# Two transformer blocks on one core: moving operands read backwards, and each chunk at another distance from its weights

## Chip, cores and metric

The kernel runs on one core of one Trainium2 chip. The metric is the device time of one execution in microseconds (us), from the first to the last instruction and what lies around it; lower is better. Two runs of the kernel before gave 3431.12 and 3433.68 us (median 3432.4).

## The reference

The reference computes two stacks of two layers each, on 512 tokens of width 1024, batch 1, everything in float32. In short:

```python
# first stack, per layer
proj = h @ w_in[l]                                    # 1024 -> 2594 columns
mixed = concat([nsa_mixer(...), gla_mixer(...), pool_mixer(...)])
h = layer_norm(ALPHA * h + mixed @ w_out[l], ...)
ff = square(relu(h @ w_up[l])) @ w_down[l]            # 1024 -> 4096 -> 1024
h = layer_norm(ALPHA * h + ff, ...)
# second stack, per layer
h = h + 0.5 * rms_norm(swiglu(rms_norm(h), ffn_wi, ffn_wo))   # 1024 -> 2 x 2816 -> 1024
h = h + rms_norm(attention(rms_norm(h)))              # dilated heads in layer 0, windowed GQA in layer 1
h = h + 0.5 * rms_norm(swiglu(rms_norm(h), ffn_wi, ffn_wo))
h = h + rms_norm((p @ ple_proj) * sigmoid(rms_norm(h) @ ple_gate))
```

Nearly all the arithmetic is in the dense products, which is where the change works.

## The kernel before

Everything is kept transposed: features lie on the 128 partitions, and the 512 tokens lie along the free dimension. The hidden state h is 8 chunks of 128 features. A dense product is therefore a sum over chunks kc: the stationary operand is a 128x128 block of weights, the moving operand is chunk kc of the activations with its 512 tokens (2048 bytes in each partition), and the result fills one PSUM bank of 512 float32.

The products are done in the type float32r, which rounds its operands. To keep float32 accuracy each operand is split in two: a high part (the value rounded to float32r) and a low part (the value minus the high part). Each product then takes three matmuls: high weights by high activations, high weights by low activations, low weights by high activations. This is `piece` (L870 to L876), the helper through which nearly all dense work goes; `abreast` (L910 to L928) does the same for the first tiles behind a norm, where the chunks of x come one at a time, with the three matmuls on L918, L919 and L925.

**Activations.** Three buffers hold split activations: `x` (8 chunks; input of the projections and of the first half of each feed-forward, and also the mixer's output in the first stack), `mid` (22 chunks; the hidden layer of the feed-forwards) and `px` (2 chunks; the embedding, inside x's memory). In the attention stages of the second stack `ao` and `bo` play the part of mid. Each chunk holds the 512 high values and behind them the 512 low values, so a chunk is 4096 bytes in each partition. ScalarE (ACT) writes the high part with a copy (L1589, L1606, L1672, L1803, L1850, L1861, L1881), VectorE (DVE) the low part by a subtraction (`lo_of` L2042, L2071, L2095, L2583).

**Weights.** The host lays all weights out as a stream of units of 128x1024 float32: 8 blocks of 128 columns, so block kc begins kc times 512 bytes into its unit. SyncE fetches them in order into 4 buffers `raw`; ACT makes the high part `wh` (L1549) and DVE the low part `wl` in the place of raw (L2026). Ten units go into a buffer apart (`wh_apart`, `wl_apart`), so that more of them are ready when a norm ends.

**Where things lie.** Buffers have hand-made addresses. `x` begins at byte 32896, a chunk and a weight unit are multiples of 512 bytes, and two lines pad `mid` and `bo` so that they too begin at the same residue:

```python
place[0] += (x_at - place[0]) % 512
mix_at = place[0]
mid = at("mid", [P, FF2C, 2, S], F32R)
```

So in the kernel before the first byte of every moving row of 2048 bytes and the first byte of every block of weights have the same address modulo 512.

**Order of the work.** Each engine has its own program written out by hand, with semaphores between them. TensorE runs through the units; in the mixer stages the small matmuls of the attention are woven in between the dense ones by plans (`plan_n`, `plan_a`, `plan_b`). At the end of each layer part a norm needs the whole result, and the first tiles behind it run `abreast`.

Of the kernel before, what the change touches and what calls it, by code (L numbers as in the profile page):

```python
# [25 lines left out]
P = 128  # L26
S = 512
# [10 lines left out]
BIG_NEG = -1.0e30  # L38
FLOOR = -1.0e20


# [347 lines left out]
def build(nc, stream, x_t, p_t, small, vecs, tab1, tab_a, tab_b, consts, out):  # L389
    n_units = stream.shape[0]  # L390
    with ExitStack() as ctx:
        place = [16512]

        def at(name, shape, dt=F32, offset=None):
# [5 lines left out]
            return nc.alloc_sbuf_tensor_at(name, shape, dt, offset=offset)  # L400

        def sem(name):
            s = ctx.enter_context(nc.semaphore(name))
            return s
# [3 lines left out]
        x_at = place[0]  # L408
        x = at("x", [P, DC, 2, S], F32R)
        y_at = place[0]  # L410
        y = at("y", [P, DC, S])
        px = at("px", [P, 2, 2, S], F32R, offset=x_at + 6 * 2 * S * 4)
        raw = [at(f"raw{i}", [P, UNIT]) for i in range(4)]
# [13 lines left out]
        mix_at = place[0]  # L427
        mid = at("mid", [P, FF2C, 2, S], F32R)
        assert place[0] <= 229368, place[0]
# [438 lines left out]
        def _(pe):  # L868
            c = Count(pe)

            def piece(dst, u, col, src, kc, start, stop):

                hi, lo = high_of(u)[:, col:col + P], low_of(u)[:, col:col + P]
                pe.matmul(dst, hi, src[:, kc, 0, :], start=start, stop=False)  # L874
                pe.matmul(dst, hi, src[:, kc, 1, :], start=False, stop=False)  # L875
                return pe.matmul(dst, lo, src[:, kc, 0, :], start=False, stop=stop)  # L876

# [32 lines left out]
            def abreast(u, t, kc, width, summed=True):  # L910


                if t == 0:
                    c.wait(x_hi)
                at_ = slice(kc * P, kc * P + P)
                hi, lo = high_of(u + t)[:, at_], low_of(u + t)[:, at_]
                dst = bank[c.homes[t][0]][:, :]
                pe.matmul(dst, hi, x[:, kc, 0, :], start=kc == 0, stop=False)  # L918
                pe.matmul(dst, lo, x[:, kc, 0, :], start=False, stop=False)  # L919
                if t < width - 1:  # L920
                    return
                c.wait(x_ready)
                for i in range(width):
                    dst, hi = bank[c.homes[i][0]][:, :], high_of(u + i)[:, at_]
                    mm = pe.matmul(dst, hi, x[:, kc, 1, :], start=False, stop=kc == 7)  # L925
# [610 lines left out]
        def _(act):  # L1536
# [47 lines left out]
            def layer_norm(g, b, to_x, after=None, wide=False):  # L1584
                for k in range(DC):
                    c.wait(normed)
                    bias = vec[:, b + k:b + k + 1]
                    if to_x:
                        act.activation(x[:, k, 0, :], prod[k % 2][:, :], ACT.Identity, bias=bias).then_inc(x_hi, 1)  # L1589
# [79 lines left out]
            for k in range(DC):  # L1669
                if k % 2 == 0:  # L1670
                    act.wait_ge(h_in[k // 2], 16)
                act.activation(x[:, k, 0, :], h[:, k, :], ACT.Copy).then_inc(x_hi, 1)  # L1672
            split(2)
            act.wait_ge(consts_in, 48)

            for layer in range(DEPTH):
# [47 lines left out]
                for stage, k in plan_n(BY_TWO if layer else BY_ONE):  # L1724
# [40 lines left out]
                    elif stage == "mixed":  # L1765
                        if k == 0:
                            c.wait(go_out)
                            c.wait(pool_read, 2)
                        ch = (GO, GO + 1, GO + 2, PU, PU + 1)[k]
                        act.activation(x[:, 3 + k, 0, :], proj[:, ch, :], ACT.Copy).then_inc(mx_hi, 1)  # L1770
                    elif stage == "exps":
                        exps(*k)
                    elif stage == "blocks":
                        copy_blocks(*k)
                    elif stage == "shift":
                        c.tick("group1")
                        act.wait_ge(blk_turned, c.n["group1"])
                        act.activation(tmp[1][:, :], bank[6][:, :], ACT.Copy).then_inc(blk_read, 1)
                    elif stage == "out":
                        act.wait_ge(o_done, 12 * layer + 4 * k + 4)  # L1780
                        act.activation(x[:, k, 0, :], bank[7][:, :], ACT.Copy).then_inc(ot_hi, 1)
                c.tick("shifted", DC)
# [13 lines left out]
                def up4(i, counts=()):  # L1796
                    for k in range(4):
# [40 lines left out]
            def ffn2(embed=False):  # L1838
                def two(i, counts=()):
                    for k in range(2):  # L1840
# [8 lines left out]
                        c.wait(pair_made)  # L1849
                        act.activation(mid[:, i * 2 + k, 0, :], prod[k][:, :], ACT.Copy).then_inc(mid_hi, 1)  # L1850

# [6 lines left out]
                if embed:  # L1858
                    c.wait(p_in, 16)
                    for k in range(2):  # L1860
                        act.activation(px[:, k, 0, :], pf[:, k, :], ACT.Copy).then_inc(p_hi, 1)  # L1861
                    c.wait(p_ready, 2)
# [28 lines left out]
            def mixer_a():  # L1891
                c.start(banks_mixer)
                for stage, k in plan_a():
# [22 lines left out]
                    elif stage == "out":  # L1916
                        out_hi(ungrouped(ao[:, k, 0, :]), grouped_src(bank[7][:, :]), k)
                rest(1)
# [9 lines left out]
            def mixer_b():  # L1928
                c.start(banks_mixer)
                for stage, k in plan_b():  # L1930
# [21 lines left out]
                    elif stage == "out":  # L1952
                        out_hi(bo[:, k, 0, :], bank[7][:, :], 4 + k)
                rest(4)
# [62 lines left out]
        def _(dve):  # L2017
# [27 lines left out]
            def layer_norm(g, to_x, wide=False):  # L2045
# [22 lines left out]
                for k in range(DC):  # L2068
                    if to_x:
                        c.wait(x_hi)  # L2070
                        dve.scalar_tensor_tensor(x[:, k, 1, :], prod[k % 2][:, :], vec[:, g + 8 + k:g + 9 + k],  # L2071
                                                 x[:, k, 0, :].bitcast(F32), ALU.add, ALU.subtract).then_inc(x_ready, 1)
                        c.tick("made x_ready")
# [18 lines left out]
            def low_part(g, k):  # L2092

                c.wait(x_hi)
                dve.scalar_tensor_tensor(x[:, k, 1, :], h[:, k, :], vec[:, g + k:g + k + 1],  # L2095
                                         x[:, k, 0, :].bitcast(F32), ALU.mult, ALU.subtract).then_inc(x_ready, 1)
                c.tick("made x_ready")
# [268 lines left out]
            for k in range(DC):  # L2366
                c.wait(x_hi)
                lo_of(x[:, k, 1, :], h[:, k, :], x[:, k, 0, :], x_ready)
            split(2)
# [8 lines left out]
            for layer in range(DEPTH):  # L2378
                c.start(banks_first)
                for stage, k in plan_n(BY_TWO if layer else BY_ONE):  # L2380
# [46 lines left out]
                    elif stage == "mixed":  # L2427
                        ch = (GO, GO + 1, GO + 2, PU, PU + 1)[k]
                        c.wait(mx_hi)
                        lo_of(x[:, 3 + k, 1, :], proj[:, ch, :], x[:, 3 + k, 0, :], x_ready)  # L2430
                    elif stage == "values_in":
# [16 lines left out]
                    elif stage == "out_lo":  # L2448
                        c.wait(ot_hi)
                        dve.tensor_tensor(x[:, k, 1, :], bank[7][:, :], x[:, k, 0, :].bitcast(F32),  # L2450
                                          ALU.subtract).then_inc(ot_ready, 1)
# [25 lines left out]
                def up4(i, counts=()):  # L2477
                    for k in range(4):
# [42 lines left out]
            def ffn2(embed=False):  # L2521
                def two(i, counts=()):
                    for k in range(2):
# [7 lines left out]
                        c.wait(mid_hi)  # L2531
                        lo_of(mid[:, i * 2 + k, 1, :], prod[k][:, :], mid[:, i * 2 + k, 0, :], mid_ready)

# [5 lines left out]
                if embed:  # L2539
                    for k in range(2):  # L2540
                        c.wait(p_hi)
                        lo_of(px[:, k, 1, :], pf[:, k, :], px[:, k, 0, :], p_ready)
                for k in range(DC):
# [72 lines left out]
            def mixer_a():  # L2616
                trig(grouped(tba[:, A_COS:A_COS + S]), grouped(tba[:, A_SIN:A_SIN + S]), regrouped(rs_in[:, :]))
                c.start(banks_mixer)
                for stage, k in plan_a():
# [29 lines left out]
                    elif stage == "out_lo":  # L2649
                        out_low(ungrouped(ao[:, k, 1, :]), grouped_src(bank[7][:, :]), ungrouped(ao[:, k, 0, :]), k)  # L2650
                rest(1)
# [19 lines left out]
            def mixer_b():  # L2671
                trig(tbb[:, B_COS:B_COS + S], tbb[:, B_SIN:B_SIN + S], rs_in[:, :])
                c.start(banks_mixer)
                for stage, k in plan_b():
# [247 lines left out]
```

## Time and profile before

| | us |
|---|---|
| runs, not profiled | 3431.12 and 3433.68, median 3432.4 |
| the profiled execution, its own time | 3430.66 |
| its span, first to last instruction | 3428.8 |
| TensorE matmul busy | 3317.4, 97% |
| VectorE busy | 1836.8, 54% |
| ScalarE busy | 1241.6, 36% |

The mean granted clock of TensorE is 0.988 of full speed. The busy time of a matmul covers its whole way through the array, and matmuls overlap: one of 512 columns is shown as 390 ns long while the next begins some 227 ns after it. So the distance from start to start tells the pace, and the busy time does not.

### The profile page before, as it was taken

What the parts mean: (1) busy time and instruction counts of PE and PEld (TensorE: products, weight loads), DVE (VectorE), ACT (ScalarE), POOL (GpSimd) and SP (SyncE); (2) the same over time, 40 slices, a digit from 0 to 9 for tenths busy, and PEclk for the clock granted to TensorE, in tenths of its full rate; (3) what the DMA queues carried; (4) which work ended last, traced back from release to release, by engine and by line L of the source; (5) the groups of instructions that cost most, each with busy time, mean ns of one, the idle gap of its engine ahead of it and who ended that gap; (6) DMA issues with size and microseconds to landing.
All of it is one profiled execution on the core that took longest, in us unless ns stands there. A gap on an engine that the chain in (4) does not pass through costs nothing.

```text
span 3428.8 us, 42531 instructions
## 1 busy us (share of the span) xinstructions
PE 3317.4 (97%) x16570; PEld 2633.9 (77%) x16570; DVE 1836.8 (54%) x2932; ACT 1241.6 (36%) x1878; POOL 342.3 (10%) x244
## 2 busy tenths in 40 slices
PE   9999999999899999999999999999999989999997
PEld 6667888776688887888777778887788876688886
DVE  5776334567752446443566664435644357654436
ACT  3354222424442324332333342324432235532324
POOL 0310000212100020000233100000000012100001
PEclk9999999999999999999999999999999999999999
DMA  4102222311122222223322122232222321122232
GB/s 162 62 32 74 96 95 98 128 62 50 50 85 94 98 98 81 98 97 104 107 74 68 63 81 96 98 105 93 86 96 94 105 94 39 61 98 98 98 105 80
DMA packets 81431, 300.35 MB, mean 88 GB/s; under 512 B 9040, under 2 KB 9040, under 8 KB 80640
## 3 DMA queue, kind: packets, MB, share of 16 engines
q1 hardware_dynamic: 78624, 284.20, 24.8%
q0 software_dynamic: 1568, 11.98, 0.9%
q8 instruction: 103, 1.69, 0.2%
q10 hardware_dynamic: 1088, 2.10, 0.2%
q14 instruction: 48, 0.39, 0.0%
HBM read 296.14 MB, written 2.10 MB: 87 GB/s over the span
## 4 chain that ended last, share of the span: by engine, by line
PE 88%; DVE 6%; ACT 3%; issue 1%; POOL 1%; DMA 1%; ACTq 0%; DVEq 0%; POOLq 0%
PE bank L874 25%; PE bank L876 25%; PE bank L875 24%; PE bank L918 2%; PE bank L925 2%; PE bank L919 2%; DVE wl L2026 1%; PE bank L1411 1%; ACT sc L1710 1%; PE bank L1423 1%; PE bank L1175 1%; PE bank L1156 1%; ACT wh L1549 1%; PE bank L1466 1%; PE bank L1114 1%
## 5 line engine op out<-in xcount | busy, mean ns | idle before, releaser
L874 PE MATMUL bank<-x,wh 128*128 128x512 f32 x2632 | 1053.7, 400 | 14.8 <-DVE h L2470 5.7
L876 PE MATMUL bank<-x,wl 128*128 128x512 f32 x2632 | 1027.3, 390 | 0.0
L875 PE MATMUL bank<-x,wh 128*128 128x512 f32 x2632 | 1026.1, 390 | 0.0
L1549 ACT ACTIVATE wh<-raw 128x1024 fp32r<-128x1024 f32 x528 | 558.0, 1057 | 1171.6 <-PE bank L876 1083.6
L2026 DVE TENSOR_TENSOR wl<-raw,wh 128x1024 fp32r<-128x1024 f32 x528 | 677.7, 1284 | 567.4 <-ACT wh L1549 566.0
L874 PEld LDWEIGHTS bank<-x,wh 128*128 128x128 f32 x2632 | 494.9, 188 | 135.9 <-issue 29.4
L876 PEld LDWEIGHTS bank<-x,wl 128*128 128x128 f32 x2632 | 494.6, 188 | 105.4
L875 PEld LDWEIGHTS bank<-x,wh 128*128 128x128 f32 x2632 | 495.7, 188 | 98.4 <-issue 3.4
L874 PE MATMUL bank<-mid,wh 128*128 128x512 f32 x1216 | 474.9, 391 | 0.5 <-DVE wl L2026 0.5
L876 PE MATMUL bank<-mid,wl 128*128 128x512 f32 x1216 | 473.1, 389 | 0.0
L875 PE MATMUL bank<-mid,wh 128*128 128x512 f32 x1216 | 473.1, 389 | 0.0
L874 PEld LDWEIGHTS bank<-mid,wh 128*128 128x128 f32 x1216 | 228.3, 188 | 49.5 <-DVE wl L2026 1.3
L875 PEld LDWEIGHTS bank<-mid,wh 128*128 128x128 f32 x1216 | 228.3, 188 | 48.4 <-issue 1.0
L876 PEld LDWEIGHTS bank<-mid,wl 128*128 128x128 f32 x1216 | 228.3, 188 | 47.2
L2165 DVE TENSOR_TENSOR prod<-bank,rs_in 128x512 f32<-128x512 f32 x88 | 60.8, 691 | 231.7 <-PE bank L876 231.7
L2042 DVE TENSOR_TENSOR mid<-prod,mid 128x512 f32 (+1 forms) x152 | 104.8, 690 | 88.3 <-ACT mid L1850 85.5
L677 POOL TENSOR_TENSOR acc<-sq,sq 128x512 f32<-128x512 f32 x8 | 11.2, 1397 | 1299.2 <-ACT sq L1655 1299.2
L918 PE MATMUL bank<-x,wh 128*128 128x512 f32 x200 | 85.9, 429 | 46.9 <-ACT x L1606 23.8
L2482 DVE TENSOR_TENSOR prod<-tmp,bank 128x512 f32<-128x512 f32 x64 | 44.0, 687 | 142.9 <-ACT tmp L1800 142.9
L1850 ACT ACTIVATE mid<-prod 128x512 f32 (+1 forms) x88 | 55.6, 632 | 174.6 <-DVE prod L2530 174.6
L1800 ACT ACTIVATE tmp<-bank 128x512 f32<-128x512 f32 x64 | 38.2, 596 | 178.5 <-PE bank L876 178.5
L2165 DVE TENSOR_TENSOR tmp<-bank,rs_in 128x512 f32<-128x512 f32 x88 | 60.8, 691 | 59.7 <-PE bank L876 58.6
(340 smaller groups left out, 3294.5 us busy)
## 6 DMA issues: line engine op xcount, KB each, us to landing
raw<-stream SPq DMA_DIRECT2D x528, 512.0 KB, 3.3
raw_apart<-stream SPq DMA_DIRECT2D x10, 512.0 KB, 3.6
sm<-small POOLq DMA_DIRECT2D x2, 2144.0 KB, 10.6
tb<-tab POOLq DMA_DIRECT2D x2, 1728.0 KB, 14.8
h<-x_t ACTq DMA_DIRECT2D x4, 512.0 KB, 6.8
out_t<-h SPq DMA_DIRECT2D x8, 256.0 KB, 2.1
tba<-tab_a POOLq DMA_DIRECT2D x1, 1152.0 KB, 8.5
pf<-p_t POOLq DMA_DIRECT2D x2, 512.0 KB, 3.9
```

Source lines behind the costliest of these rows:

```text
L874: pe.matmul(dst, hi, src[:, kc, 0, :], start=start, stop=False)
L875: pe.matmul(dst, hi, src[:, kc, 1, :], start=False, stop=False)
L876: return pe.matmul(dst, lo, src[:, kc, 0, :], start=False, stop=stop)
L918: pe.matmul(dst, hi, x[:, kc, 0, :], start=kc == 0, stop=False)
L919: pe.matmul(dst, lo, x[:, kc, 0, :], start=False, stop=False)
L925: mm = pe.matmul(dst, hi, x[:, kc, 1, :], start=False, stop=kc == 7)
L1549: act.activation(high_of(n)[:, :], raw_of(n)[:, :], ACT.Copy).then_inc(hi_done, 1)
L1850: act.activation(mid[:, i * 2 + k, 0, :], prod[k][:, :], ACT.Copy).then_inc(mid_hi, 1)
L2026: dve.tensor_tensor(low_of(n)[:, :], raw_of(n)[:, :], high_of(n)[:, :].bitcast(F32), ALU.subtract).then_inc(split_done, 1)
L2042: dve.tensor_tensor(dst, src, hi.bitcast(F32), ALU.subtract).then_inc(done, 1)
L2165: free(dve.tensor_tensor(dst, bank[c.peek()][:, :], rs_in[:, :], ALU.mult))
L2482: free(dve.tensor_tensor(prod[k % 2][:, :], tmp[k % 2][:, :], b[:, :], ALU.mult))
```

## The change

It edits three things, all about where and in which order the split activations lie; no instruction is added, removed or moved on any engine, and the sequences of instructions of TensorE, VectorE, ScalarE, GpSimd and SyncE are the same but for line numbers.

1. The 512 tokens of each part are stored in reverse order in x, mid, px, ao and bo, and every dense matmul reads them with a step of minus one element, from the last byte of the row to the first. The columns arrive in the array in the same order of tokens as before, so the PSUM banks and all that reads them are as they were. What writes x, px, ao and bo writes backwards; what writes mid reads its source backwards and writes forwards.
2. The chunks of x and px are 16 bytes longer than their data (X_GAP, 4 elements), those of mid 32 bytes (MID_GAP, 8 elements). Chunk kc therefore begins 16 kc bytes (x) or 32 kc bytes (mid) past the residue that its block of weights has. ao and bo get no gap.
3. The buffers behind x are shifted so that they keep x's residue modulo 512, and the feed-forward's buffer apart, which lies inside mid's memory, moves by 192 bytes.

```diff
+X_GAP, MID_GAP = 4, 8
...
+        def staggered(name, chunks, gap, offset=None):
+
+            t = at(name, [P, chunks, 2 * S + gap], F32R, offset)
+            return t[:, :, 0:2 * S].rearrange("p k (e s) -> p k e s", e=2)
+
...
-        x = at("x", [P, DC, 2, S], F32R)
+        x = staggered("x", DC, X_GAP)
+        place[0] += (x_at - place[0]) % 512
...
-        px = at("px", [P, 2, 2, S], F32R, offset=x_at + 6 * 2 * S * 4)
+        px = staggered("px", 2, X_GAP, x_at + 6 * (2 * S + X_GAP) * 4)
...
-        mid = at("mid", [P, FF2C, 2, S], F32R)
+        mid = staggered("mid", FF2C, MID_GAP)
...
-        apart_at = [mix_at + 6 * 2 * S * 4, y_at]
+        apart_at = [mix_at + 6 * (2 * S + MID_GAP) * 4, y_at]
...
-                pe.matmul(dst, hi, src[:, kc, 0, :], start=start, stop=False)
-                pe.matmul(dst, hi, src[:, kc, 1, :], start=False, stop=False)
-                return pe.matmul(dst, lo, src[:, kc, 0, :], start=False, stop=stop)
+                pe.matmul(dst, hi, src[:, kc, 0, ::-1], start=start, stop=False)
+                pe.matmul(dst, hi, src[:, kc, 1, ::-1], start=False, stop=False)
+                return pe.matmul(dst, lo, src[:, kc, 0, ::-1], start=False, stop=stop)
...
-                act.activation(x[:, k, 0, :], h[:, k, :], ACT.Copy, scale=vec[:, g + k:g + k + 1]).then_inc(x_hi, 1)
+                act.activation(x[:, k, 0, ::-1], h[:, k, :], ACT.Copy, scale=vec[:, g + k:g + k + 1]).then_inc(x_hi, 1)
...
-                        act.activation(mid[:, i * 4 + k, 0, :], prod[k % 2][:, :], ACT.Copy).then_inc(mid_hi, 1)
+                        act.activation(mid[:, i * 4 + k, 0, :], prod[k % 2][:, ::-1], ACT.Copy).then_inc(mid_hi, 1)
...
-                        lo_of(mid[:, i * 4 + k, 1, :], prod[k % 2][:, :], mid[:, i * 4 + k, 0, :], mid_ready)
+                        lo_of(mid[:, i * 4 + k, 1, :], prod[k % 2][:, ::-1], mid[:, i * 4 + k, 0, :], mid_ready)
...
-                        out_low(bo[:, k, 1, :], bank[7][:, :], bo[:, k, 0, :], 4 + k)
+                        out_low(bo[:, k, 1, ::-1], bank[7][:, :], bo[:, k, 0, ::-1], 4 + k)
```

The other edits of the diff put the same `::-1` at the three matmuls of `abreast` and at the remaining writers of x, px, ao and bo (ACT and DVE), and reverse the source at the second writer of mid.

## Rows read from the trace of the kernel before

**Rows 1.** The page, parts 1 and 2: busy time by engine, granted clock, DMA.
```profile
PE 3317.4 (97%) x16570; PEld 2633.9 (77%) x16570; DVE 1836.8 (54%) x2932; ACT 1241.6 (36%) x1878; POOL 342.3 (10%) x244
...
PEclk9999999999999999999999999999999999999999
...
DMA packets 81431, 300.35 MB, mean 88 GB/s; under 512 B 9040, under 2 KB 9040, under 8 KB 80640
```
**Rows 2.** The page, part 4: the chain that ended last, by engine and by line.
```profile
PE 88%; DVE 6%; ACT 3%; issue 1%; POOL 1%; DMA 1%; ACTq 0%; DVEq 0%; POOLq 0%
```
**Rows 3.** The page, part 5: groups of the dense matmuls and the splits.
```profile
L874 PE MATMUL bank<-x,wh 128*128 128x512 f32 x2632 | 1053.7, 400 | 14.8 <-DVE h L2470 5.7
L875 PE MATMUL bank<-x,wh 128*128 128x512 f32 x2632 | 1026.1, 390 | 0.0
L1549 ACT ACTIVATE wh<-raw 128x1024 fp32r<-128x1024 f32 x528 | 558.0, 1057 | 1171.6 <-PE bank L876 1083.6
L2026 DVE TENSOR_TENSOR wl<-raw,wh 128x1024 fp32r<-128x1024 f32 x528 | 677.7, 1284 | 567.4 <-ACT wh L1549 566.0
L874 PE MATMUL bank<-mid,wh 128*128 128x512 f32 x1216 | 474.9, 391 | 0.5 <-DVE wl L2026 0.5
```
**Rows 4.** Smaller groups by form: L874 on other buffers, L918 on x.
```profile
L918 PE MATMUL bank<-x,wh 128*128 128x512 f32 x200 | 85.9, 429 | 46.9 <-ACT x L1606 23.8 <-ACT x L1589 12.2 <-ACT x L1672 6.9
...
L918 PE MATMUL bank<-x,wh_apart 128*128 128x512 f32 x64 | 27.3, 426 | 0.0
L874 PE MATMUL bank<-bo,wh 128*128 128x512 f32 x64 | 26.8, 419 | 0.2 <-DVE bo L2583 0.2
...
L874 PE MATMUL bank<-ao,wh 128*128 128x512 f32 x32 | 14.1, 441 | 2.9 <-DVE ao L2583 2.7
...
L874 PE MATMUL bank<-px,wh 128*128 128x512 f32 x16 | 7.1, 442 | 0.0
...
L874 PE MATMUL bank<-px,wh_apart 128*128 128x512 f32 x16 | 6.2, 389 | 0.0
```
**Rows 5.** Timeline of PE, an undisturbed stretch: start us, length us, engine, instruction.
```profile
499.83 0.39 PE L874 MATMUL bank<-x,wh 128*128 128x512 f32 x1
500.06 0.39 PE L875 MATMUL bank<-x,wh 128*128 128x512 f32 x1
...
502.78 0.39 PE L875 MATMUL bank<-x,wh 128*128 128x512 f32 x1
```
**Rows 6.** Timeline of PE's weight loads in the same stretch.
```profile
499.83 0.19 PEld L875 LDWEIGHTS bank<-x,wh 128*128 128x128 f32 x1
500.06 0.19 PEld L876 LDWEIGHTS bank<-x,wl 128*128 128x128 f32 x1
```
**Rows 7.** Timeline of PE behind a norm, at half clock.
```profile
1303.39 0.76 PE L918 MATMUL bank<-x,wh 128*128 128x512 f32 x1 [4.69 <-ACT x L1606]
...
1304.38 0.63 PE L918 MATMUL bank<-x,wh_apart 128*128 128x512 f32 x1
1304.81 0.63 PE L919 MATMUL bank<-x,wl_apart 128*128 128x512 f32 x1
...
1307.37 0.63 PE L918 MATMUL bank<-x,wh 128*128 128x512 f32 x1
```
**Rows 8.** Stretches: busy us (x) of PE, PEld, DVE, ACT, POOL; PEclk, DMA share, GB/s.
```profile
500.00:503.00 3.00, 3.00 (x14) 2.46 (x14) 0.71 (x2) 0.25 (x1) 0.00 (x0) 1.00 0.00 1
1303.00:1307.00 4.00, 3.61 (x9) 2.86 (x10) 3.72 (x6) 3.94 (x7) 0.00 (x0) 0.50 0.02 4
```
**Rows 9.** Timeline of PE: dense matmuls behind a group of small ones.
```profile
720.57 0.50 PE L874 MATMUL bank<-x,wh 128*128 128x512 f32 x1
720.91 0.40 PE L875 MATMUL bank<-x,wh 128*128 128x512 f32 x1
...
721.84 0.39 PE L876 MATMUL bank<-x,wl 128*128 128x512 f32 x1
...
722.52 0.39 PE L876 MATMUL bank<-x,wl 128*128 128x512 f32 x1
```
**Rows 10.** Writers of ao and bo: instruction, count, ns min/median/max, first and last start.
```profile
L1881 ACT ACTIVATE ao<-bank x4: 597/597/597, 1802.1 to 1971.8; 128x512 fp32r<-128x512 f32 x4
L2583 DVE TENSOR_TENSOR ao<-bank,ao x4: 680/680/683, 1806.2 to 1972.6; 128x512 fp32r<-128x512 f32 x4
...
L1881 ACT ACTIVATE bo<-bank x8: 572/574/597, 2848.3 to 2961.2; 128x512 fp32r<-128x512 f32 x8
L2583 DVE TENSOR_TENSOR bo<-bank,bo x8: 685/692/692, 2848.9 to 2962.5; 128x512 fp32r<-128x512 f32 x8
```
**Rows 11.** Waits of PE, longest first: us in total, times, longest.
```profile
PE bank L918 <- ACT x L1606: 23.8, 6, 4.7
PE bank L918 <- ACT x L1589: 12.2, 3, 4.3
```

More of the change, by code:

```diff
@@ L917, in abreast @@
                 dst = bank[c.homes[t][0]][:, :]
-                pe.matmul(dst, hi, x[:, kc, 0, :], start=kc == 0, stop=False)
-                pe.matmul(dst, lo, x[:, kc, 0, :], start=False, stop=False)
+                pe.matmul(dst, hi, x[:, kc, 0, ::-1], start=kc == 0, stop=False)
+                pe.matmul(dst, lo, x[:, kc, 0, ::-1], start=False, stop=False)
                 if t < width - 1:
@@ L924, in abreast @@
                     dst, hi = bank[c.homes[i][0]][:, :], high_of(u + i)[:, at_]
-                    mm = pe.matmul(dst, hi, x[:, kc, 1, :], start=False, stop=kc == 7)
+                    mm = pe.matmul(dst, hi, x[:, kc, 1, ::-1], start=False, stop=kc == 7)
                     if kc == 7:
@@ L1588, in layer_norm @@
                     if to_x:
-                        act.activation(x[:, k, 0, :], prod[k % 2][:, :], ACT.Identity, bias=bias).then_inc(x_hi, 1)
+                        act.activation(x[:, k, 0, ::-1], prod[k % 2][:, :], ACT.Identity, bias=bias).then_inc(x_hi, 1)
                         c.tick("affine")
@@ L1671, in _ @@
                     act.wait_ge(h_in[k // 2], 16)
-                act.activation(x[:, k, 0, :], h[:, k, :], ACT.Copy).then_inc(x_hi, 1)
+                act.activation(x[:, k, 0, ::-1], h[:, k, :], ACT.Copy).then_inc(x_hi, 1)
             split(2)
@@ L1769, in _ @@
                         ch = (GO, GO + 1, GO + 2, PU, PU + 1)[k]
-                        act.activation(x[:, 3 + k, 0, :], proj[:, ch, :], ACT.Copy).then_inc(mx_hi, 1)
+                        act.activation(x[:, 3 + k, 0, ::-1], proj[:, ch, :], ACT.Copy).then_inc(mx_hi, 1)
                     elif stage == "exps":
@@ L1780, in _ @@
                         act.wait_ge(o_done, 12 * layer + 4 * k + 4)
-                        act.activation(x[:, k, 0, :], bank[7][:, :], ACT.Copy).then_inc(ot_hi, 1)
+                        act.activation(x[:, k, 0, ::-1], bank[7][:, :], ACT.Copy).then_inc(ot_hi, 1)
                 c.tick("shifted", DC)
@@ L1849, in two @@
                         c.wait(pair_made)
-                        act.activation(mid[:, i * 2 + k, 0, :], prod[k][:, :], ACT.Copy).then_inc(mid_hi, 1)
+                        act.activation(mid[:, i * 2 + k, 0, :], prod[k][:, ::-1], ACT.Copy).then_inc(mid_hi, 1)
                 c.start(banks_gated)
@@ L1860, in ffn2 @@
                     for k in range(2):
-                        act.activation(px[:, k, 0, :], pf[:, k, :], ACT.Copy).then_inc(p_hi, 1)
+                        act.activation(px[:, k, 0, ::-1], pf[:, k, :], ACT.Copy).then_inc(p_hi, 1)
                     c.wait(p_ready, 2)
@@ L1916, in mixer_a @@
                     elif stage == "out":
-                        out_hi(ungrouped(ao[:, k, 0, :]), grouped_src(bank[7][:, :]), k)
+                        out_hi(ungrouped(ao[:, k, 0, ::-1]), grouped_src(bank[7][:, :]), k)
                 rest(1)
@@ L1952, in mixer_b @@
                     elif stage == "out":
-                        out_hi(bo[:, k, 0, :], bank[7][:, :], 4 + k)
+                        out_hi(bo[:, k, 0, ::-1], bank[7][:, :], 4 + k)
                 rest(4)
@@ L2070, in layer_norm @@
                         c.wait(x_hi)
-                        dve.scalar_tensor_tensor(x[:, k, 1, :], prod[k % 2][:, :], vec[:, g + 8 + k:g + 9 + k],
-                                                 x[:, k, 0, :].bitcast(F32), ALU.add, ALU.subtract).then_inc(x_ready, 1)
+                        dve.scalar_tensor_tensor(x[:, k, 1, ::-1], prod[k % 2][:, :], vec[:, g + 8 + k:g + 9 + k],
+                                                 x[:, k, 0, ::-1].bitcast(F32), ALU.add, ALU.subtract).then_inc(x_ready, 1)
                         c.tick("made x_ready")
@@ L2094, in low_part @@
                 c.wait(x_hi)
-                dve.scalar_tensor_tensor(x[:, k, 1, :], h[:, k, :], vec[:, g + k:g + k + 1],
-                                         x[:, k, 0, :].bitcast(F32), ALU.mult, ALU.subtract).then_inc(x_ready, 1)
+                dve.scalar_tensor_tensor(x[:, k, 1, ::-1], h[:, k, :], vec[:, g + k:g + k + 1],
+                                         x[:, k, 0, ::-1].bitcast(F32), ALU.mult, ALU.subtract).then_inc(x_ready, 1)
                 c.tick("made x_ready")
@@ L2367, in _ @@
                 c.wait(x_hi)
-                lo_of(x[:, k, 1, :], h[:, k, :], x[:, k, 0, :], x_ready)
+                lo_of(x[:, k, 1, ::-1], h[:, k, :], x[:, k, 0, ::-1], x_ready)
             split(2)
@@ L2429, in _ @@
                         c.wait(mx_hi)
-                        lo_of(x[:, 3 + k, 1, :], proj[:, ch, :], x[:, 3 + k, 0, :], x_ready)
+                        lo_of(x[:, 3 + k, 1, ::-1], proj[:, ch, :], x[:, 3 + k, 0, ::-1], x_ready)
                     elif stage == "values_in":
@@ L2449, in _ @@
                         c.wait(ot_hi)
-                        dve.tensor_tensor(x[:, k, 1, :], bank[7][:, :], x[:, k, 0, :].bitcast(F32),
+                        dve.tensor_tensor(x[:, k, 1, ::-1], bank[7][:, :], x[:, k, 0, ::-1].bitcast(F32),
                                           ALU.subtract).then_inc(ot_ready, 1)
@@ L2531, in two @@
                         c.wait(mid_hi)
-                        lo_of(mid[:, i * 2 + k, 1, :], prod[k][:, :], mid[:, i * 2 + k, 0, :], mid_ready)
+                        lo_of(mid[:, i * 2 + k, 1, :], prod[k][:, ::-1], mid[:, i * 2 + k, 0, :], mid_ready)
                 c.start(banks_gated)
@@ L2541, in ffn2 @@
                         c.wait(p_hi)
-                        lo_of(px[:, k, 1, :], pf[:, k, :], px[:, k, 0, :], p_ready)
+                        lo_of(px[:, k, 1, ::-1], pf[:, k, :], px[:, k, 0, ::-1], p_ready)
                 for k in range(DC):
@@ L2649, in mixer_a @@
                     elif stage == "out_lo":
-                        out_low(ungrouped(ao[:, k, 1, :]), grouped_src(bank[7][:, :]), ungrouped(ao[:, k, 0, :]), k)
+                        out_low(ungrouped(ao[:, k, 1, ::-1]), grouped_src(bank[7][:, :]), ungrouped(ao[:, k, 0, ::-1]), k)
                 rest(1)
```

## The prediction

> **What bounds the kernel now.** I read the busy shares first. TensorE is busy 97% of the span, and the granted clock shows 9 tenths or more in every slice [rows 1]. The chain of work that ended last agrees: 88% of it is PE, 6% DVE, 3% ACT, with almost nothing for DMA [rows 2]. The groups then say which work that is: the three lines of `piece` on x and on mid, with hardly any idle time before them (14.8 us before 2632 matmuls of L874) [rows 3]. The makers of the weights are paced by TensorE and not the other way: ACT sits idle 1171.6 us before its splits, 1083.6 of it until a matmul on L876 has ended, and a unit costs ACT 1.06 us and DVE 1.28 us, while its 24 matmuls take 24 x 0.227 = 5.4 us [rows 3]. So if one dense matmul gets cheaper, nearly all of it should reach the end.
>
> What does a dense matmul cost? Not its 390 ns, which overlap. In an undisturbed stretch 13 steps lie between 499.83 and 502.78 us: 2.95 / 13 = 226.9 ns each [rows 5]. The waits of TensorE elsewhere are short (23.8 and 12.2 us in all for the longest two, both the first chunks behind a norm) [rows 11].
>
> **How much of this 227 ns could be lost time.** Behind a norm the kernel shows the same matmul at half clock (PEclk 0.50, that is 1.2 GHz, after TensorE had stood idle 4.69 us for the norm [rows 7]; 1.00, that is 2.4 GHz, in the undisturbed stretch) [rows 8]. There 7 steps take 1307.37 - 1304.38 = 2.99 us, 427 ns each [rows 7]. 512 columns at 1.2 GHz are 426.7 ns: at half clock a step is its columns and nothing else. At full clock the same 512 columns are 213.3 ns, and the step is 226.7: 13.4 ns are lost in each, 32 cycles, only when the array runs fast. Something that is fast enough at half clock is too slow at full clock.
>
> What it might be shows in two places. The weight load of the next matmul starts in the same hundredth of a microsecond as the moving stream of the present one [rows 5, 6], so both are reading SBUF side by side. And the loss is not the same everywhere: behind a group of small matmuls the first 4 full steps take 721.84 - 720.91 = 0.93 us, 232.5 ns each, and then 3 steps take 722.52 - 721.84 = 0.68 us, 226.7 each, with the same operands' buffers and the same residues of their addresses [rows 9]. A fixed price of each instruction would not depend on how the two streams stand to each other in time. I take this as a sign, no proof, that the two reads hinder each other and that the loss depends on which addresses they are at when. The change alters just that: the direction in which the moving row is walked, and its distance to the weights.
>
> **The change part by part.**
>
> Count of matmuls it touches: L874 has 2632 (x), 1216 (mid) [rows 3], 64 (bo), 32 (ao), 16 + 16 (px) [rows 4], together 3976; L875 and L876 have as many each, so 11,928. `abreast` has 200 + 64 on L918 [rows 4] and as many on each of its other lines, 792. Sum 12,720. Of these, some run at half clock, where nothing is lost: the mean clock of 0.988 means 2.4% of 3428.8 us, 82 us, at most 82 / 0.427 = 190 matmuls. Others stand first behind small matmuls, where the step is 0.34 us (720.57 to 720.91 [rows 9]) for another reason: the mean of L874 on x is 10 ns above that of L875 [rows 3], 26 us in all, or about 240 such places at 0.11 us. I count 12,720 - 430 = about 12,300.
>
> Price for each step at full clock. Lower end: all lost time goes, 13.4 ns, -165 us. Upper end: each step becomes as the disturbed ones, 232.5 ns, +5.8 ns, +71 us; I see no row that would bear out more. The nearest row for "another relation of the two reads" is that of rows 9, but it is on the bad side, and the kernel's relation is one among many, so some distances will be better and some worse. Two things pull to the better side. Walking both in one direction, if the load walks from its last column, makes them meet less often than walking against each other; and 8 distances of 16 bytes (22 of 32 in mid) mean that no matmul repeats one bad relation for the whole product. I take half of the loss away: 220.1 ns, -6.6 x 12,300 = -81 us.
>
> The Trainium skill says the opposite in "SBUF — State Buffer", section "Who interferes with whom": the moving operand and the weight load have independent read ports and TensorE never waits on anyone. "TensorE: Matmul & The Clock Gate", part 1, gives a warm step as N / 2.4 + about 2.5 ns, which is 215.8 for 512 columns. The trace agrees with its cold step (427) and not with its warm one (226.7); it would give the change nothing if the ports were all there is, and -10.9 x 12,300 = -134 us if the excess over its figure is what the change removes.
>
> The writers. The reversed stores and loads of ACT and DVE add no instruction. The nearest rows: for ao, ACT reads its bank with steps of 128 elements and takes 597 ns, against 572 to 597 for bo, which reads straight; DVE takes 680 against 685 to 692 [rows 10]. So order costs these engines nothing beyond noise; at most 25 ns on each of about 100 chunk writes behind norms, where TensorE waits, 2.5 us. I take 0.
>
> Moved buffers and the gaps add no work. No queue or wait changes place. What is late next if steps shrink by 3%: the split of a unit (1.28 us on DVE) against 5.3 us of matmuls still has room, and the fetches run at a mean of 88 GB/s [rows 1] with peaks that TensorE nowhere waits for long [rows 11]. The waits behind norms stay as they are.
>
> **Sum.** Profiled execution 3430.7 us, less 81, is 3350; the median of the runs is 1.7 us above the profiled one. I predict 3350 us.
>
> **Rivals.**
>
> *All of the loss goes.* The new relation never meets, and the step falls to nearly its columns, 216 ns: -10.7 x 12,300 = -132 us, 3299 us. For it: the half-clock rows show that the loss can be absent. Against it: that is at another ratio of time to column, and the new distances are many, so some should still meet.
>
> *The loss is not a read conflict.* If 32 cycles are a fixed price of changing weights, hidden at half clock, then direction and distance change nothing: 3431 us. For it: the steps on x and on mid, on the high and the low part, are all the same 227 ns, with a stability that a conflict would not need to have. Against it: the 232.5 of rows 9. But before, every operand had the same residue, so sameness is what a conflict would show too.
>
> *The distances are worse than the common one.* Before, all operands had one residue, and the step locked at 226.7 after a few matmuls; when each chunk begins elsewhere, the two streams never settle and each step costs what the four steps of rows 9 do: +5.8 x 12,300 = +71 us, 3502 us. It decides from the point where the mean step goes above 226.7; at 232.4 it is 2%. For it: rows 9 are the only look at unsettled steps, and all of them are slow. Against it: they stand behind small matmuls with other weights, where the first load is late.
>
> **How the numbers follow.** Chances: part of the loss goes (step 217 to 224 ns, 3310 to 3398 us) 0.45; all goes 0.16; nothing changes 0.26; worse 0.13. Within 2% of 3432 is about what a measurement of this kernel can tell from no change. The bound of faster is 3364 us, a step of about 221.3. Of the first case I put 0.28 below it and 0.17 above. Faster: 0.28 + 0.16 = 0.44. Slower by over 2%: 0.08 of the worst case's 0.13. Same: 0.17 + 0.26 + 0.05 = 0.48. The range runs from 3290, just under the second case, to 3450, which takes in no change and a slight loss and leaves out the worst case; the likeliest case's own range is 3310 to 3398.
>
> **What would show it right or wrong.** The step in the undisturbed stretches: 220 if right, 227 if there is no conflict, 216 if all goes. If distance matters, steps should differ by chunk within a unit, and between x and mid; if only direction does, all steps are the same and bo, which has no gap, shows it as well. The half-clock steps must stay at 427. The durations of the writers on ACT and DVE should stay within 25 ns. The prediction is wrong if the steps shrink but idle time of PE grows by as much, which would mean that a supplier of weights or chunks was nearer than I read.

## The result and the profile after

The changed kernel takes 3505.7 us (3505.06 and 3506.36), the kernel before 3432.4 us (3431.12 to 3433.68). The ratio is 1.0215, 95% interval 1.019 to 1.0239: slower by 2.15%, 73 us; whether by more or less than 2% the interval leaves open. The profiled execution has a span of 3503.3 us, 74.5 us more than before.

The page of the changed kernel, parts 1, 4 and 5 (columns as in [rows 1 to 3]):

```profile
PE 3398.3 (97%) x16570; PEld 2638.3 (75%) x16570; DVE 1833.8 (52%) x2932; ACT 1239.8 (35%) x1878; POOL 339.8 (10%) x244
...
PE 90%; DVE 5%; ACT 3%; issue 1%; POOL 1%; DMA 1%; ACTq 0%; DVEq 0%; POOLq 0%
...
L881 PE MATMUL bank<-x,wh 128*128 128x512 f32 x2632 | 1074.8, 408 | 11.8 <-DVE wl L2033 5.3
...
L882 PE MATMUL bank<-x,wh 128*128 128x512 f32 x2632 | 1047.8, 398 | 0.0
L1556 ACT ACTIVATE wh<-raw 128x1024 fp32r<-128x1024 f32 x528 | 556.8, 1055 | 1231.7 <-PE bank L883 1139.4
L2033 DVE TENSOR_TENSOR wl<-raw,wh 128x1024 fp32r<-128x1024 f32 x528 | 676.7, 1282 | 585.9 <-ACT wh L1556 584.6
...
L881 PE MATMUL bank<-mid,wh 128*128 128x512 f32 x1216 | 486.0, 400 | 0.0
```

The reader is to see that everything is as in [rows 1 to 3] except the dense matmuls. Counts, the durations of the splits and the shares of the other engines stand still; TensorE is 81 us longer busy, each dense matmul is shown 8 to 9 ns longer, and ACT's idle time until a matmul on L883 (L876 before) has grown by 56 us. So TensorE slowed down by itself, and the others wait for it.

The timeline of PE in the same undisturbed stretch, to be held against [rows 5]:

```profile
499.73 0.40 PE L883 MATMUL bank<-x,wl 128*128 128x512 f32 x1
...
502.77 0.40 PE L881 MATMUL bank<-x,wh 128*128 128x512 f32 x1
```

There are 13 steps between the two, 3.04 us, 233.8 ns each, against 226.9 before. Behind a norm at half clock nothing has changed, 6 steps in 1329.99 - 1327.43 = 2.56 us, 427 ns each, as in [rows 7], at a granted clock of 0.50:

```profile
1327.43 0.63 PE L926 MATMUL bank<-x,wl_apart 128*128 128x512 f32 x1
...
1329.99 0.63 PE L925 MATMUL bank<-x,wh 128*128 128x512 f32 x1
```

The backward writers cost nothing: the writer of x behind a norm takes 723 ns against 724 on the same form before, its partner on DVE 751 and 751; the writers of bo are those of [rows 10]:

```profile
L2102 DVE SCALAR_TENSOR_TENSOR x<-h,vec,x 128x512 fp32r<-128x512 f32 x64 | 48.1, 751 | 5.1 <-ACT x L1613 2.1
L1613 ACT ACTIVATE x<-h,vec 128x512 fp32r<-128x512 f32 x64 | 46.3, 723 | 63.4 <-DVE h L2125 63.1
```
```profile
L1888 ACT ACTIVATE bo<-bank x8: 572/574/597, 2909.5 to 3022.6; 128x512 fp32r<-128x512 f32 x8
L2590 DVE TENSOR_TENSOR bo<-bank,bo x8: 683/691/692, 2910.1 to 3023.9; 128x512 fp32r<-128x512 f32 x8
```

**The whole difference in one number.** In the trace, 11,614 matmuls of `piece` follow directly on another. About 11,310 of these steps are under 245 ns (the rest lie at half clock, behind small matmuls or behind a wait). Their mean is 227.14 ns before and 233.90 after: 6.76 x 11,310 = 76 us, against the 74.5 us by which the span grew. Nothing else needs explaining. What remains is which part of the change did it.

### The profile page after: what moved, and what is told of

Its sections match the earlier page's. It is cut to its first block, busy times and chain, and to the rows that moved or that the text cites. A ratio compares the mean times of both kernels' runs of the same rounds, so it can differ in the third digit from the quotient of the medians.

```text
span 3503.3 us, 42531 instructions
## 1 busy us (share of the span) xinstructions
PE 3398.3 (97%) x16570; PEld 2638.3 (75%) x16570; DVE 1833.8 (52%) x2932; ACT 1239.8 (35%) x1878; POOL 339.8 (10%) x244
## 4 chain that ended last, share of the span: by engine, by line
PE 90%; DVE 5%; ACT 3%; issue 1%; POOL 1%; DMA 1%; ACTq 0%; DVEq 0%; POOLq 0%
PE bank L881 26%; PE bank L883 25%; PE bank L882 25%; PE bank L925 2%; PE bank L926 2%; PE bank L932 2%; DVE wl L2033 1%; PE bank L1418 1%; ACT sc L1717 1%; PE bank L1430 1%; PE bank L1182 1%; PE bank L1197 1%; PE bank L1473 1%; PE bank L1121 1%; PE bank L1163 1%
## 5 line engine op out<-in xcount | busy, mean ns | idle before, releaser
L881 PE MATMUL bank<-x,wh 128*128 128x512 f32 x2632 | 1074.8, 408 | 11.8 <-DVE wl L2033 5.3
L883 PE MATMUL bank<-x,wl 128*128 128x512 f32 x2632 | 1048.4, 398 | 0.0
L882 PE MATMUL bank<-x,wh 128*128 128x512 f32 x2632 | 1047.8, 398 | 0.0
L883 PEld LDWEIGHTS bank<-x,wl 128*128 128x128 f32 x2632 | 495.6, 188 | 120.6
L881 PE MATMUL bank<-mid,wh 128*128 128x512 f32 x1216 | 486.0, 400 | 0.0
L882 PE MATMUL bank<-mid,wh 128*128 128x512 f32 x1216 | 483.0, 397 | 0.0
L883 PE MATMUL bank<-mid,wl 128*128 128x512 f32 x1216 | 483.0, 397 | 0.0
L883 PEld LDWEIGHTS bank<-mid,wl 128*128 128x128 f32 x1216 | 228.6, 188 | 56.5
L925 PE MATMUL bank<-x,wh 128*128 128x512 f32 x200 | 87.0, 435 | 46.3 <-ACT x L1613 23.7
```

The costliest lines, as they stand in the source:

```text
L881: pe.matmul(dst, hi, src[:, kc, 0, ::-1], start=start, stop=False)
L882: pe.matmul(dst, hi, src[:, kc, 1, ::-1], start=False, stop=False)
L883: return pe.matmul(dst, lo, src[:, kc, 0, ::-1], start=False, stop=stop)
L925: pe.matmul(dst, hi, x[:, kc, 0, ::-1], start=kc == 0, stop=False)
```

## The experiments

The theory going in was that of the prediction, turned round: the moving read and the weight load get in each other's way, and the loss depends on their direction and distance. Rivals: only the changing distances cost (the prediction's third rival); only the direction costs; or each matmul pays a fixed price.

Two kinds of result follow. A whole kernel gives its time. A kernel of matmuls alone (experiments 3, 7 and 8) was run once each, and what counts there is the step inside it.

**1. Reversal alone.**

```diff
-X_GAP, MID_GAP = 4, 8
+X_GAP, MID_GAP = 0, 0
```

> The changed kernel with both gaps set to 0: tokens reversed, chunks at the old distance. If the direction of the moving read is what costs, the undisturbed step is 233 ns in every chunk and the time is 3432 + 12,300 x 6.6 ns = about 3513 us, no better than the changed kernel's 3506. If the distances cost (my rival of the prediction: the two reads never settle), the step is back at 226.7 ns and the time at 3432 us.

Measured: 3501.0 us (3500.21 to 3502.85), ratio 1.0205 (1.0188 to 1.0222). So reversal alone brings 70 of the 73 us. Its mean step is 233.38 ns, 6.24 ns more than before, and 6.24 x 11,313 steps are 71 us.

**2. Gaps alone.** All `::-1` of the changed kernel are taken out again, the gaps stay.

```diff
-                pe.matmul(dst, hi, src[:, kc, 0, ::-1], start=start, stop=False)
+                pe.matmul(dst, hi, src[:, kc, 0, :], start=start, stop=False)
```

> The changed kernel with all tokens in forward order again: only the gaps of 16 and 32 bytes stay. If the direction costs, the time is 3432 us within 10 us, with steps that may differ by chunk by a few ns either way. If the distances cost, it is about 3506 us and the step 233 ns or more. If distances alone were the better half of the change, it is below 3400 us.

Measured: 3486.8 us (3485.03 to 3488.16), ratio 1.016 (1.0143 to 1.0177). Here neither expectation held. The gaps are not harmless: alone they cost 56 us (mean step 232.07 ns, 4.93 x 11,305 = 56 us). So both parts of the change are bad, and they do not add: 70 + 56 would be 126, and together they cost 73.

The same 100 us of the trace, from 2100 on, where TensorE does nothing but `piece` on x, shows it in counts: PE's row of the stretch view in the kernel before, the changed one, reversal alone and gaps alone (us, busy us, count, PEclk, DMA share, GB/s).

```profile
2100.00:2200.00 100.00, 100.00 (x443) 1.00 0.30 100
```
```profile
2100.00:2200.00 100.00, 100.00 (x429) 1.00 0.28 94
```
```profile
2100.00:2200.00 100.00, 100.00 (x430) 1.00 0.28 92
```
```profile
2100.00:2200.00 100.00, 100.00 (x432) 1.00 0.28 94
```

443 matmuls in 100 us at full clock before, 429 after; reversal alone 430, gaps alone 432. Step by step, reversal alone gives 233 or 234 ns in 11,075 of 11,313 steps, the same in every chunk: a locked value, as 226.7 was before. With gaps alone the steps differ from chunk to chunk, from 225 to 239 ns. With both, x's first chunks are at 233 to 234 and chunk 6, with the first two matmuls of chunk 7, at 235 to 237.

One buffer separates the two parts inside each kernel: bo is read backwards but has no gap. At the end of the last attention stage 86 matmuls on bo follow each other without a pause. The first and the last row of that group, in the kernel before, the changed one and gaps alone:

```profile
2963.56 0.39 PE L875 MATMUL bank<-bo,wh 128*128 128x512 f32 x1
...
2982.86 0.39 PE L876 MATMUL bank<-bo,wl 128*128 128x512 f32 x1
```
```profile
3025.00 0.40 PE L882 MATMUL bank<-bo,wh 128*128 128x512 f32 x1
...
3044.83 0.40 PE L883 MATMUL bank<-bo,wl 128*128 128x512 f32 x1
```
```profile
3009.95 0.39 PE L882 MATMUL bank<-bo,wh 128*128 128x512 f32 x1
...
3029.24 0.39 PE L883 MATMUL bank<-bo,wl 128*128 128x512 f32 x1
```

Between the two rows lie 85 steps: 227.1 ns each before, 233.3 in the changed kernel, 226.9 with gaps alone, where bo is forward and unmoved. So bo slowed through its direction, and the gaps of the other buffers did nothing to it.

**3. The disputed cost by itself.** A kernel of its own loads x and one unit of weights, splits nothing, computes no part of the reference and then runs the three matmuls of `piece` over 8 chunks, 24 to a case, one line of code to a case, with nothing else running.

```python
o = kc * (2 * S + gap) + d
xh, xl = mov[:, o:o + tok], mov[:, o + S:o + S + tok]
if rev:
    xh, xl = xh[:, ::-1], xl[:, ::-1]
hi, lo = wh[:, kc * P:kc * P + cols], wl[:, kc * P:kc * P + cols]
```

> No part of the reference is computed: two short loads, then only dense matmuls like those of piece, 24 to a case, on one moving buffer, with the moving row forward or reversed, at 32 distances of 16 bytes from the weights' residue (and 4, 8, 12, 24 bytes), with gaps of 16 to 128 bytes from chunk to chunk, with fewer weight columns (32, 64, 96) and with fewer tokens (256, 384). If the two reads hinder each other, the step at full clock changes with the distance (between 216 and 236 ns) and the loss over the columns' own 213.3 ns shrinks with fewer weight columns (13.4 ns at 128, about 7 at 64, 3 at 32). If the loss is a fixed price of each matmul, the step is 226.7 forward at every distance and with any number of weight columns; and if the reversed read has a fixed price, 233.3 in all its cases.

The timeline of PE, first row of each of some cases (L69 forward at 0 bytes, L71 at 16, L127 at 464; L159 reversed at 0, L175 at 128):

```profile
29.15 0.62 PE L69 MATMUL bank<-mov,wh 128*128 128x512 f32 x2
...
34.59 0.62 PE L71 MATMUL bank<-mov,wh 128*128 128x512 f32 x2
...
40.15 0.63 PE L73 MATMUL bank<-mov,wh 128*128 128x512 f32 x2
...
190.62 0.62 PE L127 MATMUL bank<-mov,wh 128*128 128x512 f32 x2
...
196.25 0.62 PE L129 MATMUL bank<-mov,wh 128*128 128x512 f32 x2
...
275.63 0.63 PE L159 MATMUL bank<-mov,wh 128*128 128x512 f32 x2
...
281.23 0.63 PE L161 MATMUL bank<-mov,wh 128*128 128x512 f32 x2
...
320.45 0.63 PE L175 MATMUL bank<-mov,wh 128*128 128x512 f32 x2
...
326.12 0.63 PE L177 MATMUL bank<-mov,wh 128*128 128x512 f32 x2
```

From row to row lie 24 steps. L69 to L71: 5.44 / 24 = 226.7 ns, the kernel's own value, so this small kernel shows the same thing. L71: 5.56 / 24 = 231.7. L127: 5.63 / 24 = 234.6. Reversed, L159: 5.60 / 24 = 233.3; L175: 5.67 / 24 = 236.3. The mean steps of the 23 starts to starts inside each case, by distance:

```
bytes      0    16    32    48    64    80    96   112   128   144   160   176   192   208   224   240
forward 226.7 231.4 233.5 233.1 229.3 230.8 233.7 231.2 232.7 233.4 233.8 233.2 233.0 234.4 232.9 227.0
+256    228.3 231.5 233.5 233.1 229.3 230.8 233.8 231.2 232.7 233.4 233.7 233.2 233.0 234.3 232.9 227.0
reversed 233.3 233.3 233.3 233.3 233.3 233.3 233.7 233.6 236.5 233.2 233.4 233.4 233.3 233.3 233.4 236.5
```

Three things follow. Forward, the step does depend on the distance, with a period of 256 bytes, and the kernel before stood at the lowest of all values. Reversed, it hardly does: 233.3, or 236.5 at 128 and 240 bytes, and these two came out at 233.2 to 233.6 in the later sweeps. And rows that do not begin on a multiple of 16 bytes are at 237.9 (4 bytes) and 229.5 (12) forward, 235.6 and 241.5 reversed, with 8 and 24 bytes between these. With 32, 64 and 96 instead of 128 weight columns the forward step was 231.5, 230.1 and 230.0, and the reversed one 233.3 in all three. The expected shrinking of the loss with the columns did not come; forward the loss was larger.

The cases ran in rising order of distance in both rows of the table, and experiment 8 shows that a step can also depend on what ran before. So each entry is one value that its case can take. With neither operand moved and 128 weight columns, every case of the three sweeps with rows of 512 tokens that began at full clock ended at 226.7.

**4. One common distance in the whole kernel**, forward, no gaps, with the worst value of the table. px and mid get the same helper, and the buffer apart inside mid moves by 512 bytes, which keeps its residue; ao and bo stay.

```diff
+SHIFT = 52
...
+        def shifted_by(name, chunks, gap, offset=None):
+
+            t = at(name, [P, chunks * 2 * S + gap], F32R, offset)
+            return t[:, gap:].rearrange("p (k e s) -> p k e s", e=2, s=S)
+
-        x = at("x", [P, DC, 2, S], F32R)
+        x = shifted_by("x", DC, SHIFT)
```

> The kernel before, tokens in forward order, with x, px and mid moved together by one common distance of 208 bytes from the weights' residue (ao and bo stay). The sweep showed 234.4 ns for this distance against 226.7 at 0. If the sweep's loss is the kernel's loss, the step is 234.4 ns in all chunks and the time is 3431 + about 12,200 x 7.7 ns = 3525 us. If what costs in the kernels with gaps is that the distance changes from chunk to chunk, a common distance costs nothing and the time is 3431 us.

Measured: 3508.9 us (3500.74 to 3511.76), ratio 1.0226 (1.0209 to 1.0243). The mean step of the profiled execution (3500.7 us) is 233.83 ns. So a common distance costs as much as a changing one: the sweep's loss is the kernel's loss, though its size came out 16 us under the 3525 expected. In the unwoven stretches steps were at 234.5 to 234.7 for most of the trace and lower early on: the means of its first three tenths are 232.6, 230.6 and 233.6. The four runs of this kernel also lie 11 us apart, while those of the kernel before beside it lie within 4 (3430.48 to 3433.69).

**5. The control, 256 bytes in place of 208.**

```diff
-SHIFT = 52
+SHIFT = 64
```

> The kernel of shift_all with the common distance 256 bytes in place of 208: the control for its moved buffers. The sweeps showed the same steps at d and d + 256, so 226.7 ns and 3431 us, within 10 us. If moving the buffers itself costs (or their residue modulo 512 counts), it is as slow as shift_all, about 3505 us.

Measured: 3432.0 us (3427.63 to 3433.7), ratio 0.9999 (0.999 to 1.0009). The buffers are moved and the apart buffer too, and nothing is lost. 48 bytes more or less in the distance decide over 77 us.

**6. Reversed, at the common distance of 208 bytes.** The helper of experiment 4 in the kernel of experiment 1.

> Tokens reversed, no gaps, and x, px and mid at the common distance of 208 bytes, which cost 77 us in forward order. If the backward read has its own price that does not depend on the weights' address, the step is 233.3 ns and the time 3501 us, as with reversal alone. If direction and distance both act through the same meeting of two reads, or simply add, the time moves: 3570 us if they add.

Measured: 3501.2 us (3499.36 to 3502.56), ratio 1.0204 (1.0187 to 1.0221), to the microsecond that of reversal alone. The distance that costs 77 us forward costs nothing once the row is read backwards. The same stretch as above, for experiments 4, 5 and 6:

```profile
2100.00:2200.00 100.00, 100.00 (x428) 1.00 0.28 94
```
```profile
2100.00:2200.00 100.00, 100.00 (x443) 1.00 0.30 99
```
```profile
2100.00:2200.00 100.00, 100.00 (x430) 1.00 0.28 93
```

**7. Who is the other party?** Again matmuls alone, with the weights moved as well.

> Again only dense matmuls, 24 to a case, no part of the reference. Forward: moving rows and weights moved by the same distance (4 to 240 bytes); the weights moved alone (16 to 240); moving rows at 228 to 252 bytes; the low rows alone; 16, 32, 64 or 96 weight columns, the last ones of the block. Reversed: weights alone, moving rows at 228 to 252, fewer columns. If the partner is the weight load, only the difference of the two addresses counts: moved together the step is 226.7 everywhere, and weights moved by d give what moving rows at 256 - d gave (229.3 at 192, 233.7 at 160). If the moving row's own address counts (its place in a line or bank), then moving both gives what the moving row alone gave in the first sweep (231.4 at 16, 234.4 at 208), and weights moved alone change nothing. With 16 weight columns a read conflict should leave at most an eighth of the loss of 13.4 ns; a loss that has nothing to do with the load stays whole.

```
forward, bytes             96    128    160    208
moving rows alone       233.7  232.7  233.8  234.4   (experiment 3)
weights alone           234.0  233.5  233.2  233.3
both together           226.7  226.7  226.7  230.1   (once settled)
```

Moved together by any multiple of 32 bytes the step settles at 226.7, at odd multiples of 16 mostly at 230.1 (16 itself at 233.3, and at 231.0 in experiment 8), and at 4 bytes at 237.5. It takes no more than one row out of place: with the low rows alone moved by 16 to 240 bytes the step was 229.5 to 235.3. So forward it is the address of the moving row relative to the weights that counts, and the place of both in a unit of 32 bytes besides. Weights moved alone by d did not give what moving rows at 256 - d gave in all cases (233.2 at 160 against 233.7 at 96; but 231.7 at 80 against 233.2 at 176), so the exact law stays open. But the loss does not shrink with the amount that the load reads. With 16 weight columns, whose loads are shown 95 ns long against 188 for 128 columns, the forward step was 231.8 and the reversed one 233.4 (first rows of the cases, 24 steps each: 5.56 and 5.61 us):

```profile
279.13 0.63 PE L161 MATMUL bank<-mov,wh 128*16 128x512 f32 x2
...
284.69 0.63 PE L163 MATMUL bank<-mov,wh 128*32 128x512 f32 x2
...
396.65 0.63 PE L203 MATMUL bank<-mov,wh 128*16 128x512 f32 x2
...
402.26 0.63 PE L205 MATMUL bank<-mov,wh 128*32 128x512 f32 x2
```

Forward the number of columns is not without effect. With the last 32 columns alone the curve over the distance is flatter: 230.9, 230.7, 229.8, 231.5 and 228.2 ns at 0, 32, 96, 160 and 240 bytes, against 226.7, 233.5, 233.7 and 233.8 at the first four with 128 columns. Such a load also begins 384 bytes further on, and no case separates the two. And reversed, weights moved alone by 16 to 240 bytes left the step at 233.3 in all 6 cases.

**8. Length, and what ran before.**

> Only dense matmuls, 24 to a case, no part of the reference. Forward and reversed with 512, 448, 384, 320, 256 and 192 tokens: if the backward read streams at a lower rate, its loss over the columns' own time grows with the tokens (20 ns at 512, 15 at 384, 10 at 256), while the forward loss is about the same at all lengths (12 to 14 ns); if both are prices of an instruction, both stay flat. The same case (forward, moving rows at 240 bytes) behind different cases: it was 227.0 in the first sweep and 236.0 in the second; if the step depends on what ran before, both values appear again here, and if on the buffers' places, only one does. Forward and reversed with both buffers moved by the same distance: 226.7 forward at multiples of 32 bytes, 230.1 at odd multiples of 16, as before; reversed 233.3 throughout.

Loss per matmul over the columns' own time at 2.4 GHz, from the settled steps:

```
tokens            256    320    384    448    512
forward step    120.0  146.7  173.3  202.7  226.7
forward loss     13.3   13.4   13.3   16.0   13.4
reversed step   118.3  146.7  177.8  206.7  233.3
reversed loss    11.6   13.4   17.8   20.0   20.0
```

```profile
29.34 0.62 PE L71 MATMUL bank<-mov,wh 128*128 128x512 f32 x2
34.78 0.57 PE L73 MATMUL bank<-mov,wh 128*128 128x448 f32 x2
...
71.25 0.40 PE L91 MATMUL bank<-mov,wh 128*128 128x256 f32 x2
...
74.09 0.36 PE L93 MATMUL bank<-mov,wh 128*128 128x192 f32 x2
```

The first two rows are the forward case of 512 tokens (5.44 us), the last two the reversed one of 256 (2.84 us, 118.3 ns a step). From 256 to 512 tokens the forward loss is one price for each matmul, but for the row of 448. The reversed loss is larger in long rows: rows of 256 and 320 tokens lose nothing against forward, 512 tokens lose 6.6 ns. That speaks against a longer start. It does not come out as a steady lower rate of the stream either, which was expected to give 10, 15 and 20 ns at 256, 384 and 512 tokens: 384 tokens lose 17.8, and from 448 to 512 nothing is added. At 192 tokens both directions stand at 111.7 ns, and so does a forward row of 128 (experiment 7), though their columns take 80 and 53.3 ns: below 256 tokens something other than the columns sets the pace.

The second question had a clear answer: the forward case at 240 bytes ran at 226.7 ns behind the case at 236 bytes and at 233.3 behind those at 0, 224 and 16, and kept its value through 24 more matmuls; in the first sweep it was 227.0, in the second 236.0. The same instructions on the same addresses can settle at more than one pace, by what ran before. The case just before does not decide it alone: in the second sweep, too, it was that of 236 bytes.

No step of any full row of 512 columns in the three sweeps settled below 226.7, in either direction. So none of the tried addresses and directions beats the layout of the kernel before.

## Why the prediction was wrong

- *What bounds the kernel* was right. The whole difference came through the step of the dense matmuls, and 6.76 ns on some 11,310 of them gives the span's change within 2 us. The count of 12,300 was some 9% above these 11,310, which leave out what `abreast` does at full clock.
- *The sign of the change in the step* is what failed, in the words "I take half of the loss away: 220.1 ns". Measured were 233.9. The prediction's own upper end, the disturbed steps of [rows 9] at 232.5, was the nearest row and almost the answer; it was set aside with two arguments that no row bore out.
- The first argument, that walking in one direction makes the two reads meet less often, fell with experiments 1, 6 and 7: reversed, the step does not care where the weights are or how many columns they have. The backward read has a price of its own, which rows of 256 and 320 tokens do not pay. In which direction the load walks, on which the argument rested, no run shows.
- The second, that many distances spread the risk, fell with experiments 2 and 3. Among 16 distances only 0 and 240 are cheap, and 240 not in every run (233.3, 236.0). From a best point, spreading can only lose: the mean of the table's first 8 forward values is 231.2, and x in gaps alone ran at 231.9.
- "So sameness is what a conflict would show too" was right, and the next thought was missing: with every operand at one residue, the profile showed one point of a curve. Whether it was a high or a low point could not be read from it, and the unsettled steps of [rows 9], slow in the mean, spoke for a low one, though not as a proof (single steps of this kernel go down to 224 ns).
- *The rival that came true in size*, "the distances are worse than the common one" (3502 us), had the right sign for the gaps, but not their mechanism and not the cause of the change. It took the changing from chunk to chunk for the cost, and experiment 4 lost as much with one common distance. The distances bring 56 us alone, not 71, and only 4.7 us on top of the reversal, a difference within the intervals. That its 3502 us lie near the 3505.7 measured is chance.
- *The sign named beforehand*, that bo shows a cost of direction although it has no gap, did appear: 227.1 before, 233.3 after.
- *The writers at nothing* and *half clock untouched* were right (751 and 751 ns; 427 ns).
- On the Trainium skill's rule of independent ports ("SBUF — State Buffer", section "Who interferes with whom"): by it no distance could matter; experiments 4 and 5 differ in the distance alone by 77 us, so here the measurement decides against it. It shows that the addresses count, not that the two reads share a port. The Trainium skill's warm step of 215.8 ns ("TensorE: Matmul & The Clock Gate", part 1) was not reached by any case with these float32r operands.

What stays open: what the 13.4 ns are that the best forward step still loses. They depend on the relation of two addresses and do not shrink with the amount of weights read, and no run here had matmuls without a weight load. Why a backward stream is slower, and why the loss has several settled values, was not traced further.

## What to carry to other kernels

When a stream of equal instructions is a few per cent slower than its columns, measure the loss as a curve over the layout (a small kernel with one case to a line) before changing a layout that happens to be uniform: one profile shows one point, and it may be the best. For float32r rows of 512 tokens with a weight load before each matmul, keep moving rows and weights at a common residue modulo 256 bytes, begin both on a multiple of 32 bytes, and read forward. Two harmful edits may hide in each other, so undo each alone.

## What the runs showed that was not expected

- A backward read of 512 float32r tokens by TensorE costs 233.3 ns against 226.7, and at 256 tokens nothing more than forward (118.3 against 120.0).
- 208 bytes of common distance between moving rows and weights cost 77 us in 3432 (2.3%), 256 bytes cost nothing (ratio 0.9999).
- The step of one and the same case settled at 226.7, 233.3 or 236.0 ns (mean of a case) depending on what ran before, and the kernel at 208 bytes varied by 11 us from run to run.
- Loading 16 weight columns in place of 128 does not shorten the step at 512 tokens (231.8 forward, 233.4 reversed), though each load is shown 95 ns long in place of 188.
